# A hybrid encoder block on one Trainium2 core: the experts' gate and up product as three f16 products

## The reference

```python
p_sel, g_sel = lax.top_k(softmax(u @ group_w + group_b), 1)      # 4 groups
top_logits, top_idx = lax.top_k(logits of that group, 2)         # 8 experts each
...
h = silu(xb @ w_gate[e]) * (xb @ w_up[e])      # 1024 -> 256, twice
y = h @ w_down[e]                              # 256 -> 1024
out = zeros.at[token].add(y * gate)
```

## Time and profile before

| | |
|---|---|
| median of 3 runs | 3636.52 us (3635.08 to 3637.32) |
| the profiled execution | 3640.01 us, its span 3638.4 us |
| mean granted clock | 0.966 |
| PE busy | 3323.7 us (91%) |
| DVE busy | 2113.6 us (58%) |
| ACT busy | 1420.7 us (39%) |
| POOL busy | 876.3 us (24%) |
| PE, L1730, gate and up | 588.6 us busy, 1328 records |
| PE, L573, projections | 980.1 us busy, 15840 records |

### The profile page before, as it was taken

How to read it: one execution, slowest core, us unless ns; L and a number is a source line. 1 busy time by engine, 2 the same in 40 slices (tenths; PEclk the granted TensorE clock), 3 DMA queues, 4 the chain that set the end, 5 groups by cost and what they waited for, 6 DMA issues and landing times. The chain is left out here.

```text
span 3638.4 us, 81997 instructions
## 1 busy us (share of the span) xinstructions
PE 3323.7 (91%) x29622; PEld 2488.6 (68%) x29623; DVE 2113.6 (58%) x6074; ACT 1420.7 (39%) x3087; POOL 876.3 (24%) x986
## 2 busy tenths in 40 slices
PE   2888999999999999999999999995699999999980
PEld 2887788888878887888888788874344444444430
DVE  5777777777767777777777677774222222222214
ACT  4545554454445445544544454444111111111105
POOL 3322122122212112221222121121233333333320
PEclk8899999999999999999999999997799999999995
DMA  6000010001000100100010001004376766666739
GB/s 225 7 7 13 31 37 31 31 31 37 25 31 31 37 25 31 37 31 31 31 37 25 31 31 37 25 19 185 93 231 196 222 170 184 173 183 185 218 72 375
DMA packets 81097, 313.86 MB, mean 86 GB/s; under 512 B 14609, under 2 KB 14738, under 8 KB 68498
## 3 DMA queue, kind: packets, MB, share of 16 engines
q1 hardware_dynamic: 44722, 202.58, 15.3%
q0 software_dynamic: 29216, 89.30, 10.7%
q10 hardware_dynamic: 6848, 17.12, 1.2%
HBM read 212.94 MB, written 96.01 MB: 85 GB/s over the span
## 5 line engine op out<-in xcount | busy, mean ns | idle before, releaser
L573 PE MATMUL pj<-uT,W 128*128 128x128 f16 x15840 | 980.1, 220 | 27.9 <-issue 27.9
L573 PEld LDWEIGHTS pj<-uT,W 128*128 128x128 f16 x15840 | 935.5, 98 | 78.8 <-issue 73.1
L1730 PE MATMUL bA<-W,uT 128*128 x1328 | 588.6, 596 | 6.2 <-issue 3.6
L1730 PEld LDWEIGHTS bA<-W,uT 128*128 128x128 f32 x1328 | 248.1, 192 | 287.8 <-issue 287.7
L1795 DVE TENSOR_TENSOR W<-W,bA 128x256 f32<-128x256 f32 x83 | 35.0, 421 | 555.6 <-ACT W L1761 555.6
L1717 PE MATMUL pj<-W 128*128 x664 | 298.8, 593 | 0.9 <-ACT W L1766 0.9
L1478 POOL TENSOR_TENSOR dec<-tri,g 128x512 f32<-128x512 f32 x33 | 34.3, 1039 | 1026.1 <-DVE g L1234 1026.1
L1761 ACT ACTIVATE W<-bA 128x256 f32<-128x256 f32 x83 | 31.9, 384 | 535.4 <-PE bA L1730 535.4
L648 PE MATMUL bA<-dec,Mt 128*128 128x128 f32 x1584 | 224.2, 285 | 15.9 <-DVE dec L1207 14.1
L659 PE MATMUL bB<-X,qh 128*128 128x128 f32 x1584 | 222.6, 284 | 3.3 <-ACT qh L875 3.3
L648 PEld LDWEIGHTS bA<-dec,Mt 128*128 128x128 f32 x1584 | 194.5, 193 | 23.4 <-DVE dec L1207 21.3
(11 more groups left out here) (403 smaller groups left out, 5950.1 us busy)
## 6 DMA issues: line engine op xcount, KB each, us to landing
W<-w_gate SPq DMA_DIRECT2D x32, 1024.0 KB, 4.9
W<-w_up SPq DMA_DIRECT2D x32, 1024.0 KB, 8.0
W<-w_down SPq DMA_DIRECT2D x32, 1024.0 KB, 12.2
x_in<-xm SPq DMA_DIRECT2D x33, 512.0 KB, 3.6
ht<-xm SPq DMA_DIRECT2D x32, 512.0 KB, 3.6
h_rows<-ht SPq DMA_DIRECT2D x32, 512.0 KB, 2.7
u_rows<-ht SPq DMA_DIRECT2D x32, 512.0 KB, 4.1
W<-h_rows SPq DMA_DIRECT2D x32, 512.0 KB, 6.7
```

The costliest lines, as they stand in the source:

```text
L573: mm = pe.matmul(pj[g % 2][:, j, :], w16[:, k, w_half(w_high, COL[GROUPS[g]], 512, j * P, P)], (ul if low_u else uh)[:, k, :], start=(k == ...
L1730: mm = pe.matmul(bA[:].rearrange("p a b -> p (a b)").rearrange("p (g f) -> p g f", g=2), xT[:, k, :], w[:, k], start=(k == 0), stop=(k == ...
```

## The change

The gate and up product of each block becomes three products of f16 halves, high x by high w, high x by low w, low x by high w, 24 matmuls of 512 columns in all, accumulated in the same bank. x is turned as before; ACT takes its high half (times 512), DVE its low half. The weights are split by each block for the block after: `high_part` on ACT and `low_part` on DVE, 8 pieces of 128x512 each, into one of two buffers `wx`. The weights' scale, ffn_norm over the expert's root of squares, comes from a table `etab`, and its inverse goes into the sigmoid's scale and the gate. To fill the table, the mixer takes each expert's sum of squares of w_gate and w_up: SP loads them in 8 chunks of 256 KB into the two halves of ht (`raw_chunks`), ACT squares each with a sum (`raw_squares`), DVE adds the 8 sums. Some tiles of the expert stage move to other buffers, and some semaphores are merged; neither adds an instruction or a wait.

```diff
@@ Step.__init__
+        self.sums = range(1) if not isinstance(i, int) or 3 <= i < TILES - 1 else {-1: range(1), 0: range(2)}.get(i, range(0))
+        if isinstance(i, int) and i < 3:
+            self.first, self.squares, self.summed = {-1: (NE - 3, 0, 0), 0: (NE - 2, KT, 1)}.get(i, (0, 0, 0))
+        else:
+            self.first, self.squares, self.summed = i - 3, KT * i, i
@@ mixer, sync
+                def raw_chunks(s):
+                    if isinstance(s.i, int) and s.i == -1:
+                        sp.wait_ge(sem("idx_zeroed"), ZEROED)
+                    for n in s.sums:
+                        for c in range(KT):
+                            if c > 1 or n:
+                                need(sp, sem("w_sq"), s.squares + KT * n + c - 1)
+                                settle(sp)
+                            src = (w_gate, w_up)[c // 4][bass.ds(s.first + n, 1)].rearrange("o (p k) f -> p (o k f)", k=KT)
+                            sp.dma_start(ht[:, 512 * (c % 2):512 * (c % 2) + 512], src[:, 512 * (c % 4):512 * (c % 4) + 512]
+                                         ).then_inc(sem(f"w_raw{c % 2}"), 16)
...
                     if s.O:
                         need(sp, sem("u_stored"), 16 * s.nR)
                         settle(sp)
+                    raw_chunks(s)
+                    if s.O:
+                        if s.sums:
+                            need(sp, sem("w_sq"), s.squares + KT)
+                            settle(sp)
...
                         sp.dma_start(ht[:], xm[bass.ds(s.nO * P, P), :]).then_inc(sem("x_res"), 16)
@@ mixer, scalar
+                def raw_squares(s, *chunks):
+                    for part in chunks:
+                        for q in range(part * len(s.sums), (part + 1) * len(s.sums)):
+                            n, c = q // KT, q % KT
+                            need(act, sem(f"w_raw{c % 2}"), 8 * s.squares + 16 * (KT // 2 * n + c // 2 + 1))
+                            if c == 0 and n == 0:
+                                need(act, sem("w_sum"), s.summed)
+                            nc.scalar.activation(ht[:, 512 * (c % 2):512 * (c % 2) + 512], ht[:, 512 * (c % 2):512 * (c % 2) + 512], ACT.Square,
+                                                 accum_out=sqc[:, n, c:c + 1]).then_inc(sem("w_sq"), 1)
@@ mixer, scalar, body (step -1: squares 0 to 5 after the weight groups 3 to 5, then 6 and 7)
                     evac(s, 2, "k")
+                    if s.G:
+                        raw_squares(s, 0)
...
                         a.then_inc(sem("r_gate"), 1)
+                    if s.G:
+                        raw_squares(s, 1)
                     level_y(s, 5)
...
                         nc.scalar.activation(aa, yg[:], ACT.Square).then_inc(sem("y_sq"), 1)
+                    if s.G:
+                        raw_squares(s, 2)
...
                         a.then_inc(sem("i_gate"), 1)
+                    if s.G:
+                        raw_squares(s, 3)
...
                         nc.scalar.activation(th, la, ACT.Tanh, scale=-1.0).then_inc(sem("th_ready"), 1)
+                    if s.G:
+                        raw_squares(s, 4)
                     level_y(s, 6)
+                    if s.G:
+                        raw_squares(s, 5)
                     evac(s, 3, "v")
+                    if s.G:
+                        raw_squares(s, 6)
                     nc.scalar.preload_act_table_set("gelu_apprx_tanh_and_others")
...
                     nc.scalar.preload_act_table_set("silu_and_others")
+                    if s.G:
+                        raw_squares(s, 7)
@@ mixer, vector, end of body
+                    for n in s.sums:
+                        need(dve, sem("w_sq"), s.squares + KT * (n + 1))
+                        nc.vector.tensor_reduce(fsum[:, bass.ds(s.first + n, 1)], sqc[:, n, :], AX, ALU.add).then_inc(sem("w_sum"), 1)
@@ experts, tensor
-                    pe.wait_ge(sem("xT_ready"), b + 1)
+                    pe.wait_ge(sem("x_high"), b + 1)
+                    pe.wait_ge(sem("wx_high"), KT * b + KT)
                     need(pe, sem("hm_ready"), b)
-                    for k in range(KT):
-                        mm = pe.matmul(bA[:]..., xT[:, k, :], w[:, k], start=(k == 0), stop=(k == KT - 1))
+                    for part, x in ((0, uh), (1, uh), (0, ul)):
+                        if part == 1:
+                            pe.wait_ge(sem("wx_low"), b + 1)
+                        if x is ul:
+                            pe.wait_ge(sem("xT_ready"), b + 1)
+                        for k in range(KT):
+                            mm = pe.matmul(flat(bA), x[:, k, :], wx[par][:, part, k, :], ...)
@@ experts, scalar
+                def high_part(b, par):
+                    e1 = act.value_load(blk[0:1, bass.ds(3 * b, 1)], min_val=1, max_val=NE)
+                    raw = raw_of(act, b)
+                    act.wait_ge(sem("w_ready"), e1)
+                    act.wait_ge(sem("ecol_ready"), b + 1)
+                    need(act, sem("gu_full"), b - 1)
+                    for k in range(KT):
+                        nc.scalar.activation(part_of(wx[par][:, 0], k), raw[:, k], ACT.Copy,
+                                             scale=ecol[par][:, k:k + 1]).then_inc(sem("wx_high"), 1)
+                def x_part(b):
+                    act.wait_ge(sem("xg_turned"), b + 1)
+                    need(act, sem("gu_full"), b)
+                    ...  (two copies of bO times 512 into uh)
                 def body(b, par, last):
+                    if not last:
+                        high_part(b + 1, 1 - par)
                     act.wait_ge(sem("gu_full"), b + 1)
-                    nc.scalar.activation(sm, flat(bA)[:, 0:FE], ACT.Sigmoid).then_inc(sem("silu_sig"), 1)
+                    nc.scalar.activation(sm, flat(bA)[:, 0:FE], ACT.Sigmoid, scale=ecol[par][:, KT:KT + 1]).then_inc(sem("silu_sig"), 1)
+                    if not last:
+                        x_part(b + 1)
@@ experts, vector
+                def low_part(b, par):
+                    raw = raw_of(dve, b)
+                    for k in range(KT):
+                        dve.wait_ge(sem("wx_high"), KT * b + k + 1)
+                        a = nc.vector.scalar_tensor_tensor(out=part_of(wx[par][:, 1], k), in0=raw[:, k], scalar=ecol[par][:, k:k + 1],
+                                                           in1=part_of(wx[par][:, 0], k), op0=ALU.mult, op1=ALU.subtract)
+                    a.then_inc(sem("wx_low"), 1)
                 def body(b, par, last):
+                    if not last:
+                        columns(b + 1, 1 - par)
...
+                    if not last:
+                        low_part(b + 1, 1 - par)
                     dve.wait_ge(sem("silu_sig"), b + 1)
```

More of the change, by code:

```diff
@@ L1280, in body @@
                         need(dve, sem("th_ready"), s.nG)
[L1282 removed]
+                        nc.vector.scalar_tensor_tensor(out=hh, in0=hh, scalar=1.0, in1=th, op0=ALU.add,
                                                        op1=ALU.mult).then_inc(sem("w_ready"), 1)
[L1284 to L1285 removed]
+                        need(dve, sem("pre_full"), 4 * s.pG + 1)
+                        need(dve, sem("dec2_ready"), 2 * s.pG + 1)
                         nc.vector.tensor_tensor(Mt[:], bA[:], decb[:], ALU.mult).then_inc(sem("M_raw"), 1)
@@ L1588, in _ @@
                 nc.vector.tensor_copy(tcoli[:, 0:3], tcol[:, 2:5]).then_inc(sem("blk_ready"), 1)
+                dve.wait_ge(sem("fro_root"), 2)
+                nc.vector.tensor_tensor(etab[:, 1:NE + 1, 0:KT], fg[:].unsqueeze(1).to_broadcast([P, NE, KT]),
+                                        fro.unsqueeze(2).to_broadcast([P, NE, KT]), ALU.mult)
+                link(nc.vector.reciprocal(etab[:, 1:NE + 1, KT], fro))
+                link(nc.vector.tensor_scalar(etab[:, 1:NE + 1, KT], etab[:, 1:NE + 1, KT], 1.0 / U_SCALE, None, ALU.mult))
+                link(nc.vector.tensor_tensor(etab[:, 1:NE + 1, KT + 1], etab[:, 1:NE + 1, KT], etab[:, 1:NE + 1, KT], ALU.mult))
+            @block.tensor
+            def _(pe):
+                pe.wait_ge(sem("fro_sums"), 2)
+                pe.matmul(bA[:, 0, 0:NE], ones[:], fsum[:], start=True, stop=True).then_inc(sem("fro_full"), 1)
+            @block.scalar
+            def _(act):
+                nc.scalar.activation(junk[:, 0:KT], fg[:], ACT.Square, accum_out=fgs[:]).then_inc(sem("fro_sums"), 1)
+                act.wait_ge(sem("fro_sums"), 1)
+                nc.scalar.activation(fsum[:], fsum[:], ACT.Copy, scale=fgs[:]).then_inc(sem("fro_sums"), 1)
+                act.wait_ge(sem("fro_full"), 1)
+                nc.scalar.activation(fro, bA[:, 0, 0:NE], ACT.Ln, scale=2.0 ** -30, bias=tiny[:]).then_inc(sem("fro_root"), 1)
+                act.wait_ge(sem("fro_root"), 1)
+                nc.scalar.activation(fro, fro, ACT.Exp, scale=-0.5).then_inc(sem("fro_root"), 1)
             @block.sync
```

113 lines of the change are left out of this document (69 added, 44 removed).

## The result

| | before | after |
|---|---|---|
| median of 5 runs beside each other | 3636.5 us (3635.1 to 3643.9) | 3662.1 us (3659.4 to 3671.9) |
| the profiled execution | 3640.0 us | 3671.9 us, its span 3670.0 |
| mean granted clock | 0.966 | 0.960 |
| first gate and up product starts at | 2578.1 us | 2701.4 us |
| from the first to the last such product | 943.3 us | 854.0 us |

The change makes the kernel slower by 25.6 us; the ratio is 1.0073, 95% interval 1.0054 to 1.0092. The forecast was 3621, so its sign was wrong, and the measured time lies inside the range. The profiled execution is the longest of its five; its span is 31.6 us longer than that of before's profile: **123.3 us lost** ahead of the first product, **89.3 won** from there to the last one, and 2.4 won behind it.

What follows compares the result with a forecast made beforehand. The prediction took TensorE to bound both stages: from the profiled 3640, less 132 in the experts, plus 117 in the mixer, gives 3625, forecast as 3621 us beside a median of 3636.5; range 3575 to 3666.

Steps and rivals of the forecast that it cites:

- The mixer's 117: Mixer: squares waiting for chunks lengthen each of 29 steps by 3.5 us, 101 us, plus 16; 117 us lost.
- the experts' 132: Expert stage: 140 us won by the faster product less 8 for the scatter chain; 132 us gained.
- step 0: Mixer's step 0, two squares at each place: 13 us late, plus 3 for the clock; 16 us lost.
- the 2.95 taken: Mixer: landing time of a 256 KB chunk, taken as 2.95 us, halfway between 2.3 and 3.6.
- the round: Mixer, two buffers: square's signal 0.73, SP's 0.2, landing and 0.05 make 3.93 us from one chunk to the next.
- The product, 1.69 us a block: Expert stage: gate and up product falls from 6.87 to 5.18 us, 140 us over 83 blocks.
- The split is hidden with 1.6 us to spare: Expert stage: VectorE has h ready at 2.7 us, TensorE wants it at 4.3; the split costs nothing.
- The scatter chain, 8 us: Expert stage, GpSimd: each scatter waits for the former to land, binding only with two-block experts or successive loads; 8 us.
- Port contention (0.06): Rival, expert stage: GpSimd's transfers stretch VectorE's low pieces, so the split isn't hidden; 3811 us, or 3671 by half; chance 0.06.
- The clock (0.04): Rival, mixer: TensorE's clock falls after the 2.1 us stall, perhaps 3 us more a step; 3708 us; chance 0.04.
- A long landing (0.20): Rival, mixer: chunks land in 3.2 to 3.6 us; at 3.6 the mixer loses 159, 3664 us; chance 0.20.
- A quick one (0.20): Rival, mixer: chunks land in 2.3 us or the stall is partly covered; a step loses 2.2, 3580 us; chance 0.20.

Runs made afterwards that it cites:

- regs_b: Changed kernel with one high piece moved behind the sigmoid, three low pieces behind h, the column copy behind y's copy, the slot's register loaded once a block: 3650.1 us.
- cols: Changed kernel with VectorE's copy of the table column for block b+2 taken behind h of block b, and two low pieces moved behind h: 3706.5 us.
- no_add: Kernel of `regs_b` without the indirect transfers that add a block's rows to h_rows: 3611.7 us.
- e_only: Changed kernel without the mixer's chunks and squares, each expert's sum of squares replaced by a constant; the expert stage's part alone: 3551.3 us.
- edge: Changed kernel with four blocks in an iteration of the experts' loop instead of two: 3653.9 us.
- no_low: Changed kernel in which VectorE makes one of the eight low weight pieces and the second product reads the high pieces: 3657.0 us.

## Why the forecast was wrong

The sign hung on the difference of two large terms. The mixer's 117 held (118.6); the experts' 132 measured 85.9 alone, and that turned the sum. That 3662 still lies in the range is luck: its upper end stood for landings of 3.6 us, which didn't come, and not for a loss among the experts.

- **The mixer, 117 us: right.** 118.6 alone, 123.3 ahead of the first product in the profile. The step was 74.9 for 75; the waits 1.8 and 1.4 on the mean for 2.1 and 1.4; step 0 cost 15 (its product L849 starts at 244.73 instead of 229.74) for 16. A chunk landed in 3.2 us (w_gate) and 3.1 (w_up), above the 2.95 taken and inside its ends, and the round was 3.85 for 3.93, so what stands between landing and the next request was cheaper than its terms (of which the 0.2 for SP and the last 0.05 stood on no row) by more than the landing was dearer. The two errors offset each other, and in that the 117 was lucky too. The Trainium skill (DMA: Bandwidth & Descriptors, "Anatomy of one DMA") would have 2.6 us for a chunk, by a fit that the page gives for transfers issued by GpSimd; SP issues these, the trace has 3.1 to 3.2, and decides.
- **The product, 1.69 us a block: right.** 5.2 us, and 9.73 for a block wherever nothing else held it.
- **"The split is hidden with 1.6 us to spare": the step that failed first.** Both loads were right: VectorE is busy 167.9 and ScalarE 141.0 of the 200 us from 3000 on, 19.7 blocks, so 8.5 and 7.2 a block for 8.7 and 7.4. The sequence wasn't: the start of ScalarE's pieces hangs on the column copy, which stands behind y's copy on VectorE, so the sigmoid came 1.4 us behind the product and not 0.7, and h 3.7 and not 2.7. And h was compared with the wrong deadline. Not the turning of h decides, 4.3 us behind the product, but the next product, which starts no sooner than 2.2 us behind h's start at the loop's edge and 1.5 to 1.6 elsewhere: h had to start 2.3 us behind the product's end and started 3.2 behind. Moving h forward (`regs_b`) gave 15.5 us back, moving it back (`cols`) cost 41.6.
- **The scatter chain, 8 us: mis-sized, 25.1 in the blocks (`no_add` against `regs_b`).** I took it as a rate, a bound only where the scatters alone need longer than TensorE. What TensorE felt were the gathers beside them: they land in 6.3 us with scatters and 4.7 without, up to 12.2 and 9.2. In the kernel before they landed as slowly (6.2, up to 12.2), and its longer blocks covered it. The prediction has no term for them.
- So the 48.5 us that went again are 15.6 that `regs_b` gives back, 25.1 that go with the scatters, and 7.8 that no run here took away, about as much as h still costs at the edges of `no_add`.
- **The rivals.** Port contention (0.06) would have stretched VectorE; it stretched the other side, see below. The clock (0.04) did fall in some steps, and it cost nothing there. A long landing (0.20) was there in part, and was not why the kernel is slower: the mixer's term held. A quick one (0.20) didn't come. No rival was about when h is wanted or about gathers, the two mechanisms that decided.

The row behind the point on the split: VectorE's h in the kernel before, in the block of the earlier trace rows whose product starts at 3002.25.

```profile
3010.27 0.48 DVE L1799 SCALAR_TENSOR_TENSOR W<-W,gcol,bA 128x256 f32<-128x256 f32 x1
```

It starts 8.0 us behind the product's start; with 2.2 that is 10.2, and the block takes 11.42. The edge was covered by 1.2 us, which is why no wait of before shows it.

The rows behind the point on the scatters: GpSimd in the changed kernel while weights load,

```profile
2785.96 1.64 POOL L1788 DMA_INDIRECT h_rows<-lath,sid  x1 [0.90 <-POOL sid L1783]
...
2797.68 0.52 POOL L1783 COPY sid<-gx 128x1 int32 x1 [7.69 <-DMA h_rows<-lath,sid]
2799.10 1.89 POOL L1788 DMA_INDIRECT h_rows<-aahh,sid  x1 [0.90 <-POOL sid L1783]
...
2801.65 1.34 POOL L1764 DMA_INDIRECT ht<-u_rows,gid  x1 [0.16 <-POOL gx L1761]
```

and TensorE in the same block:

```profile
2813.07 1.28 PE L1802 MATMUL bO<-ident,ht 128*128 128x128 f32 x8 [3.48 <-DMA ht<-u_rows,gid]
2814.14 5.24 PE L1812 MATMUL pj<-W,qs 128*128 x8
```

The scatter of 2785.96 lands 11.7 us later, the next leaves only then and the gather behind it at 2801.65, 2.6 us ahead of the product (2804.24); in the steady stretch it is 3.2 to 6.6 ahead. TensorE, through with its product, waits 3.48 us for that gather, to 11.4 us behind its issue, and then runs slowly (5.24 us for 3.60); this block takes 15.21. So at most some 4 us of the delay are the place in the queue, and a landing in 6.3 us would have been in time.

The rows behind the clock, the stretches of the mixer's step behind the wait at level 6 (columns as in the earlier trace rows):

```profile
1560.42:1561.54 1.12, 1.12 (x8) 1.06 (x9) 0.00 (x0) 0.49 (x1) 0.00 (x0) 0.88 0.43 46
1561.54:1564.10 2.56, 2.56 (x25) 2.56 (x24) 2.16 (x8) 1.66 (x6) 0.00 (x0) 0.50 0.66 182
1564.10:1566.17 2.07, 2.07 (x30) 2.06 (x29) 1.76 (x7) 1.75 (x2) 0.00 (x0) 0.86 0.06 21
```

The granted clock is 0.50, the lower level, behind 1.86 us of idle time. The slow matmuls ended just when T came, so this step, at 74.88 us, is as long as those in which TensorE kept its clock and waited 1.2 to 1.6 us for T.

## What to carry to other kernels

When an engine's work is put ahead of something that the bound engine wants, ask for the deadline of what stands behind its reader too: in a loop, the next iteration's first instruction starts a fixed time behind the last wait of this one (here 2.2 us, 0.7 of it the edge), and a profile of a kernel with slack doesn't show that. A chain of transfers has a price beyond its own rate: look at how long the transfers beside it take to land, and at how early they leave. And work that fits by busy time can still cost by its place in the queue: the chunks and squares cost 111 us at one place and 20 at another (3662.1 and 3571.2 us against `e_only`'s 3551.3).

## What the runs showed of the hardware

The loop's edge costs TensorE 0.7 us where nothing covers it: from h's start to the next product 2.22, 2.26, 2.23 and 2.27 us in four kernels across an edge, 1.60 and 1.51 inside an iteration of `edge`. Over all twelve kernels with the f16 product, no edge in blocks 5 to 79 is under 2.21 us and no other block under 1.48. The Trainium skill (Advanced Engine Details and Errata, "Control Flow Timing") gives about 0.1 us for a compare-and-branch; the Trainium skill (Runtime: NRT & Kernel Launch, "Instruction fetch mechanics") says that a taken branch can stall on instruction fetch. No run here tells what the rest of the 0.7 us is.

VectorE's pieces with both inputs in SBUF kept their 0.75 us beside GpSimd's work, and GpSimd's instructions grew. GpSimd's and VectorE's groups from 3000 to 3200 us of the changed kernel (busy us, mean ns):

```profile
L1761 POOL COPY gx<-gid 128x2 int32 x20 | 21.1, 1056 | 0.0
...
L1764 POOL DMA_INDIRECT ht<-u_rows,gid x10 | 13.4, 1338 | 1.6 <-POOL gx L1761 1.6
...
L1921 DVE SCALAR_TENSOR_TENSOR W<-W,ecol 128x512 f16<-128x512 f16 x158 | 106.5, 746 | 16.0 <-ACT W L1866 15.3 <-issue 0.8
```

and of `no_low`, with an eighth of these pieces:

```profile
L1761 POOL COPY gx<-gid 128x2 int32 x20 | 15.0, 750 | 0.8 <-DMA gid<-idx_tab 0.8
...
L1764 POOL DMA_INDIRECT ht<-u_rows,gid x10 | 9.9, 990 | 2.4 <-POOL gx L1761 1.4 <-PE bO L1802 0.9
...
L1921 DVE SCALAR_TENSOR_TENSOR W<-W,ecol 128x512 f16<-128x512 f16 x20 | 15.0, 752 | 103.2 <-ACT W L1866 103.2
```

The Trainium skill (GPSIMD Engine Reference, "Specifications") names the contention; the runs show whose time it takes here, 0.3 us of each of GpSimd's two instructions and none of VectorE's.
